# Every SBUF tensor begins at a multiple of 64 bytes, in a three-block fp32 transformer kernel

## The reference

```
x = first_block(x, ...)    # sparse attention + gated MLP, then a feed-forward of width 2816 with a convolution
x = second_block(x, ...)   # stick-breaking, forgetting, delta-rule and convolution branches, merged by gates
return third_block(x, ...) # differential and latent attention, then 32 experts, top 4

def expert_block(args):
    xb, e = args                                   # 128 token rows, one expert
    hid = xb @ w1[e] + b1[e]                       # [128,1024] @ [1024,2048]
    return clamped_swiglu(hid[:, :D_FF_3], hid[:, D_FF_3:]) @ w2[e] + b2[e]
```

## Time and profile before

| | us |
|---|---|
| median of 3 runs | 3578.89 (3578.42 to 3579.65) |
| the profiled execution | 3578.06 |
| its span, first to last instruction | 3576.2 |
| PE busy / DVE busy / ACT busy | 3237.8 / 2274.3 / 1596.3 |
| mean granted TensorE clock | 0.940 |

### The profile page before, as it was taken

How to read it: one execution, slowest core, us unless ns; L and a number is a source line. 1 busy time by engine, 2 the same in 40 slices (tenths; PEclk the granted TensorE clock), 3 DMA queues, 4 the chain that set the end, 5 groups by cost and what they waited for, 6 DMA issues and landing times. The chain is left out here.

```text
span 3576.2 us, 48314 instructions
## 1 busy us (share of the span) xinstructions
PE 3237.8 (91%) x17290; PEld 2559.4 (72%) x17290; DVE 2274.3 (64%) x2936; ACT 1596.3 (45%) x2000; POOL 270.1 (8%) x193
## 2 busy tenths in 40 slices
PE   7888899999998878999978788779999999999996
PEld 5656787878885557887747565668888888888884
DVE  4375766337552455554545484468888888888885
ACT  1263333022244622100123153357777777777773
POOL 0000000000000000000000000011222212121211
PEclk9889999999998987999988999879999999999998
DMA  5411222232221000223273100289999999999994
GB/s 166 158 31 36 82 94 103 81 117 89 77 95 65 1 2 19 88 95 106 74 309 118 36 19 27 82 313 409 385 380 373 377 376 375 378 373 384 367 384 160
DMA packets 155002, 643.86 MB, mean 180 GB/s; under 512 B 13417, under 2 KB 65897, under 8 KB 99842
## 3 DMA queue, kind: packets, MB, share of 16 engines
q1 hardware_dynamic: 144610, 603.72, 44.7%
q0 software_dynamic: 9648, 35.13, 3.6%
q10 hardware_dynamic: 624, 3.35, 0.2%
HBM read 612.22 MB, written 32.56 MB: 180 GB/s over the span
## 5 line engine op out<-in xcount | busy, mean ns | idle before, releaser
L500 DVE TENSOR_TENSOR experts_rest<-experts_weights,experts_leading 128x2048 fp32r<-128x2048 f32 x386 | 879.3, 2285 | 87.9 <-ACT experts_leading L3358 86.5
L3358 ACT CAST experts_leading<-experts_weights 128x2048 fp32r<-128x2048 f32 x387 | 728.4, 1905 | 30.3 <-PEq L3348 16.6
L506 PE MATMUL psum<-experts_leading,experts_xT_leading 128*128 128x512 f32 x1024 | 403.2, 394 | 8.4 <-DVE experts_rest L500 8.4
L507 PE MATMUL psum<-experts_rest,experts_xT_leading 128*128 128x512 f32 x1024 | 405.2, 396 | 0.0
L508 PE MATMUL psum<-experts_leading,experts_xT_rest 128*128 128x512 f32 x1024 | 403.6, 394 | 0.0
L507 PE MATMUL psum<-proj_source_rest,proj_leading 128*128 128x512 f32 (+1 forms) x656 | 256.5, 391 | 0.0
L506 PE MATMUL psum<-proj_source_leading,proj_leading 128*128 128x512 f32 (+1 forms) x560 | 220.2, 393 | 13.4 <-DVE proj_source_rest L500 13.4
L506 PEld LDWEIGHTS psum<-experts_leading,experts_xT_leading 128*128 128x128 f32 x1024 | 193.2, 189 | 53.5 <-DVE experts_rest L500 8.9
L507 PEld LDWEIGHTS psum<-experts_rest,experts_xT_leading 128*128 128x128 f32 x1024 | 193.4, 189 | 44.8
L508 PEld LDWEIGHTS psum<-experts_leading,experts_xT_rest 128*128 128x128 f32 x1024 | 193.3, 189 | 43.5
L508 PE MATMUL psum<-proj_source_leading,proj_rest 128*128 128x512 f32 (+1 forms) x560 | 218.2, 390 | 0.0
(11 more groups left out here) (732 smaller groups left out, 6496.6 us busy)
## 6 DMA issues: line engine op xcount, KB each, us to landing
experts_weights<-in_w_up SPq DMA_DIRECT2D x259, 1024.0 KB, 9.6
experts_weights<-in_w_down SPq DMA_DIRECT2D x128, 1024.0 KB, 6.7
pieces<-in_w_pieces SPq DMA_DIRECT2D x60, 512.0 KB, 3.3
ada_unit<-in_w_ada SPq DMA_DIRECT2D x12, 2048.0 KB, 18.6
merge_first<-in_w_merge SPq DMA_DIRECT2D x16, 768.0 KB, 4.4
merge_weights<-in_w_merge SPq DMA_DIRECT2D x16, 768.0 KB, 4.2
ff_up_first<-in_w_up SPq DMA_DIRECT2D x11, 1024.0 KB, 4.8
ff_up_weights<-in_w_up SPq DMA_DIRECT2D x11, 1024.0 KB, 4.7
```

The lines of the kernel that those rows point to most:

```text
L500: return dve.tensor_tensor(out, src, leading.bitcast(F32), ALU.subtract)
L506: pe.matmul(out, lh, rh, start=start, stop=False)
L507: pe.matmul(out, lh, rl, start=False, stop=False)
L3358: act.copy(leading[h % LEADING], weights.half(h)).then_inc(masked, 1)
```

## The change

`tensor` now enters a spare tensor of 32 bytes (`{name}_end`) behind each one whose end, rounded up to 32, is no multiple of 64, so that the next one starts at a multiple of 64. `high` rounds the top down to a multiple of 64 where it was 32. The spare tensors are never read or written.

```diff
+LINE = 64
...
     def tensor(self, name, shape, dtype=F32):
-        with self.nc.sbuf_tensor(name, shape, dtype) as t:
+        with ExitStack() as own:
+            t = own.enter_context(self.nc.sbuf_tensor(name, shape, dtype))
             self.byte_of[t.name] = self.nc.sbuf_base - 4 * math.prod(shape[1:])
+            if -(-self.nc.sbuf_base // 32) * 32 % LINE:
+                own.enter_context(self.nc.sbuf_tensor(f"{name}_end", [shape[0], LINE // 8], F32))
...
-        at = self.nc.sbuf_top // 32 * 32 - below - 4 * math.prod(shape[1:])
+        at = self.nc.sbuf_top // LINE * LINE - below - 4 * math.prod(shape[1:])
```

## The result

The changed kernel takes 3586.05 us (median of 16 runs, 3582.13 to 3595.45) against 3579.03 (16 runs, 3574.64 to 3583.44): ratio 1.0021, 95% interval 1.0013 to 1.0029. It is 7.0 us slower. I had forecast 3580.6 and no measurable difference; the time lies in the range (3569 to 3589), but the interval excludes no change, and its middle stands at the 0.2% that I had named as the bound.

A forecast was written before the change was run, and what follows sets the result against it. PE was taken to bound the kernel, busy 91% of the span and pacing the experts, with DVE and DMA not holding it. The terms summed to +1.7 us on the median of 3578.9: 3580.6 us, range 3569 to 3589 for 8 in 10.

The forecast's parts named there:

- DVE and ACT at nothing: All DVE and ACT work: start at a multiple of 64 or not costs the same, from softmax instructions 1 ns apart.
- The rule that places must agree modulo 256: PE's matmuls: fast when all operands have one value modulo 256; any mixture costs 4 to 7 ns a matmul.
- 64 bytes matter after all: Rival: every mixed stage goes to 226.7 ns a matmul, -19.8 us in the experts and -16 us elsewhere: 3543; chance 0.02.
- `down1`, `merge`, `ple` +4.1 us: Half of these stages' units, rest in the top slot, become mixtures: +1.2 us, +2.5 us and +0.4 us.
- `proj2` -1.4 us: `proj2` at (0, 128, 0, 192) goes from 232.2 to 231.2 ns on some 1450 matmuls: -1.4 us.
- `ff_up`, `out1`, `out2` at 0: Units in the top slot go from 232.2 to 231.2 ns, the others to 233.4: nothing within 0.2 us.
- `proj3` -1: Units in the lower slot go from 233.4 to 226.7 ns, -0.6 us, with moving-weight units at most as much again: -1 us.
- Experts at 0: Experts' 4608 matmuls at 231.0 ns have three place values before and after: 0 taken, between -19.8 and +11.1 us.
- the slower side: Rival: the experts' pace gets worse, +11.1 us, with the other terms above 3592; decides from +1.2 ns a matmul; chance 0.14.
- neither holds PE up now nor would at a slightly faster PE: DVE in the experts, 901 of 1020 us busy, has 12% of its time left, so it would not delay PE.
- bound of -19.8 us for the experts: Best case for the experts: 4608 matmuls go from 231.0 to 226.7 ns; rival of an improved pace, 3561, chance 0.12.
- DMA at 0: Landing times may change 7% with the start, -1.5 to +1.5 us where PE waits; 0 taken; DMA rival 3579, chance 0.02.

The follow-up runs named there:

- the maps: Experiment 5 and experiment 7: kernels of PE's three passes alone on constant data, operands at chosen places modulo 256; equal places about 226.7 ns, mixtures mostly slower.
- experiment 7: Second kernel of PE's three passes alone, against experiment 5: sets in another order and new sets; moving leading and rest 16 bytes apart 232.0 ns a matmul.
- Experiment 6: The changed kernel with the top slots rounded down to a multiple of 256 in place of 64: 3576.4 us, ratio 0.9993 to the kernel before.
- experiment 5: New kernel of only PE's three passes on constant data, four operands at chosen places, other engines idle: 226.7 ns a matmul for (0, 256, 0, 0), 233.3 for (0, 128, 0, 192).
- experiment 8: Kernel of PE's three passes alone, against experiment 7: one set repeated behind different sets; (0, 128, 0, 0) ran six times at 228.9 ns, three at 233.3.
- experiment 9: The kernel before with only the experts' matmul operands (weights, xT, hidden) at 128 modulo 256: 3574.8 us, ratio 0.9987.
- experiment 12: Against experiment 1's kernel, DVE writes the rest of only half of each half-unit of experts' weights, PE's instructions as many: 3534.53 us, ratio 0.9873 to the kernel before.
- experiment 1: The kernel before with every tensor of 1 KB a partition and more, but the routing's, at 128 modulo 256: 3554.94 us, ratio 0.9930.

## Why the prediction was right or wrong

- **DVE and ACT at nothing: right.** 694 and 723 ns at a multiple of 64, 691 and 722 off it.
- **The rule that places must agree modulo 256, and that 64 bytes are worth nothing: right**, and shown: 0.9930 and 0.9939 at 128 and at 224, and the maps. The rival "64 bytes matter after all" (3543) is out. The Trainium skill ("SBUF — State Buffer", Specifications) gives lines of 16 bytes as what a stride may not leave without loss; the maps differ from reading it as a rule for starts, since a rest that began 16 bytes (modulo 256) from its leading, at such a line's start, cost 5.3 ns (experiment 7).
- **`down1`, `merge`, `ple` +4.1 us: right.** From the paces +2.4 ns x 528 = +1.3, +2.0 x 1152 = +2.3, some +0.5. Experiment 6 takes them back.
- **`proj2` -1.4 us: wrong, and the step that failed.** I had priced (0, 128, 0, 192) by the unit of `proj3` at (0, 128, 0, 224), 231.2 ns, as "most like" it. It ran at 233.3 in the kernel, and at 232.9 to 233.3 in all seven sets of experiments 5, 7 and 8. Over some 1450 matmuls that is +1.6 us, 3.0 off. The nearest place is not the nearest price: 192 beside 128 and 0 is another pattern than 224.
- **`ff_up`, `out1`, `out2` at 0: wrong by the same step.** `ff_up` went from 232.2 to 233.2 over 1056 matmuls, +1.1 us, and `out1` and `out2` (232.3 and 232.2 to 233.3) +0.4.
- **`proj3` -1: right**, -1.2 over its 432 matmuls (231.2 and 233.4 by unit became 230.9 and 226.7; the later stretch with moving weights went from 230.3 to 228.0). `proj1` and `out3` at 0: right (228.8 became 228.9 and 228.7 became 228.6).
- **Experts at 0: nearly right, by luck.** The pace rose by some 0.7 ns, which times 4608 would be +3.2 us; the stage took 0.7 us more (1198.36 against 1197.63), since at a slower pace PE comes less early to what DVE writes (the late starts cost 6.8 us in place of 8.7). Where the top slots alone moved the pace rose by 1.3 ns, more than the 1.2 that I had named for the slower side, and the stage took 1.4 us more.
- **DVE "neither holds PE up now nor would at a slightly faster PE": wrong in both halves.** I had read it from a busy share of 88% and 3.1 us of waits. Counted from start to start DVE cost PE 8.7 us before, in all 32 blocks. At 227.3 ns in place of 230.9 half of the 17 us came back as waits for DVE (experiments 9 and 12). My bound of -19.8 us for the experts rested on that reading, and so did the range, which puts half of this bound on either side of the time before. Such a share says nothing about a list in which a short urgent step stands behind long ones.
- **DMA at 0: right** for PE's time, as far as the rows go: 378 and 377 GB/s in the experts, and with the tops at 128, 379. The 7% of the earlier trace rows is not all the place's: with both slots of `out3` at 128 the two pieces took 8.6 and 8.3 us, with both at 224, 8.6 and 8.2. With the top slots at a multiple of 256 (experiment 6) both took 7.6, though the second still began at 128, and the experts' pieces of `w_down` 6.0 us, where they took 6.5 to 6.9 at 128, 192 and 224. That hints at a gain from such a start, on a term that PE does not wait for; no experiment isolates it.

With the after-paces the sum is 1.3 + 2.3 + 0.5 + 1.6 + 1.1 + 0.4 - 1.2 + 0.7 = +6.7 us, and +7.0 is measured, where my sum was +1.7: the mechanism of the places was right, and of the 5 us that it was short 4.5 are the mixtures of `proj2`, `ff_up`, `out1` and `out2`. That agreement is better than the two profiles deserve. Between first matmuls of stages they differ by +2.6 us in the first feed-forward, -4.9 from `proj2` to `merge`, +1.3 in `merge`, and by +3.8 in the differential attention, and PE stood at its lower clock 427 us in the profile before and 444 us after, in other places. Such stretches also differ between kernels whose tensors up to there are the same (experiment 9: 0.96 and 0.90), so I don't put them down to the change. On average it does not lower the clock: 0.9374 over the 16 runs after, 0.9369 over 56 runs before. How the rest of the time divides over the stages stays open, and so do the 5 us that the kernel with only the top slots moved took beyond its paces and its clock.

## What to carry to other kernels

Give all operands of one matmul group the same start address modulo 256 bytes, whichever it is; rounding to a smaller unit only deals the values anew, and rounding the bottom stack and the top slots separately breaks equalities that were there by chance. Price an unseen mixture by measuring it and not by its neighbour, and expect several values. Before a faster pace is counted as gain, look at the engine that feeds it: at 89% busy, with 2.28 us steps ahead of a 0.4 us step that PE needs, DVE took back half. Count such lateness from the start of one matmul to that of the next, since the wait that the profile shows starts only where the matmul before is taken to end. The version with everything at 128 is 0.7% faster than the kernel before and needs only the two edits of experiment 1.

## What the hardware showed that I had not expected

- Three-pass matmuls of 128x512 fp32 take 226.7 to 227.2 ns each at full clock when the four operands begin at one value modulo 256 (0, 32, 64, 96, 128, 224 tried; 256, 512 and 1024 apart are as good), and 228.8 to 234.2 ns in every mixture that I tried but one; the one is 16 bytes between the moving and the stationary pair, 226.6.
- A mixture can have more than one pace. (0, 128, 0, 0) ran at 228.9, 231.2 and 233.4 ns, constant over 96 matmuls each time, with the same instructions and a full clock, and (224, 128, 224, 224) at 231.1 and 232.3; what picks the pace is not shown.
- PE's clock differs between executions of the same instructions at the same places in when it stands at 1.2 GHz: 0.96 and 0.90 over one stage, worth 2.7 us. An effect of 0.1% can't be split by stages from a single profile; the mean clocks of all runs tell whether the clock is behind it.
